# Layer 0's last two FFN output units by thirds, squares added by GpSimd, and layer 1's first norm in single blocks

## What is computed

```python
def _rmsnorm(x, g):
    xf = x.astype(F32)
    y = xf * lax.rsqrt(jnp.mean(xf * xf, axis=-1, keepdims=True) + EPS)
    return (y * g.astype(F32)).astype(x.dtype)
...
        xp = xp + g2p[:, None] * _swiglu(hp, w_ffn_gate[l], w_ffn_up[l], w_ffn_down[l])
        xs = xs + g2s[:, None] * _swiglu(hs, w_ffn_gate[l], w_ffn_up[l], w_ffn_down[l])
...
        hp = _modulate(xp, norm_mix[l], sh1p, sc1p)
        hs = _modulate(xs, norm_mix[l], sh1s, sc1s)
...
            q, k, v = _odd_project(hp, w_in_odd[o])
```

## Time and profile before

| | us |
|---|---|
| median of 3 runs | 3015.53 |
| lowest and highest | 3014.42 and 3015.95 |
| the profiled execution | 3010.81 |
| its span in the trace | 3009.0 |
| PE busy | 2855.7 |
| DVE, POOL, ACT busy | 1745.3, 1539.7, 1007.9 |

### The profile page before, as it was taken

How to read it: one execution, slowest core, us unless ns; L and a number is a source line. 1 busy time by engine, 2 the same in 40 slices (tenths; PEclk the granted TensorE clock), 3 DMA queues, 4 the chain that set the end, 5 groups by cost and what they waited for, 6 DMA issues and landing times. The chain is left out here.

```text
span 3009.0 us, 61068 instructions
## 1 busy us (share of the span) xinstructions
PE 2855.7 (95%) x24985; PEld 2653.3 (88%) x24985; DVE 1745.3 (58%) x3132; ACT 1007.9 (33%) x2102; POOL 1539.7 (51%) x1381
## 2 busy tenths in 40 slices
PE   6999999997789999999999999999999999999998
PEld 4859999765689999999999999956699999999998
DVE  6399999556646644335697400066648543445785
ACT  3351111356434433332232311155525333332222
POOL 2121224464523877776576232144334777775675
PEclk8999999998999999999999999999999999999999
DMA  6716763642241121224222223163221222223321
GB/s 218 253 69 226 249 228 117 183 159 90 94 166 50 64 86 65 86 86 136 87 71 86 81 98 105 53 203 112 69 98 40 82 72 78 86 73 128 122 69 69
DMA packets 192053, 338.85 MB, mean 113 GB/s; under 512 B 27784, under 2 KB 107424, under 8 KB 189920
## 3 DMA queue, kind: packets, MB, share of 16 engines
q1 hardware_dynamic: 138832, 266.50, 26.4%
q10 hardware_dynamic: 52944, 68.45, 6.6%
HBM read 268.30 MB, written 79.49 MB: 116 GB/s over the span
## 5 line engine op out<-in xcount | busy, mean ns | idle before, releaser
L109 PE MATMUL tr_acc<-tr_quad_hi,ah_ring_hi 128*128 128x264 f32 x2432 | 694.7, 286 | 8.3 <-DVE tr_kept L1440 2.2
L733 POOL TENSOR_TENSOR ah_ring_lo<-ah_raw,ah_ring_hi 128x512 fp32r<-128x512 f32 (+2 forms) x426 | 579.7, 1368 | 236.9 <-ACT ah_ring_hi L1140 146.1
L111 PE MATMUL tr_acc<-tr_quad_hi,ah_ring_lo 128*128 128x264 f32 x2432 | 692.9, 285 | 0.0
L110 PE MATMUL tr_acc<-tr_quad_lo,ah_ring_hi 128*128 128x264 f32 x2432 | 690.5, 284 | 0.0
L109 PEld LDWEIGHTS tr_acc<-tr_quad_hi,ah_ring_hi 128*128 128x128 f32 x2432 | 458.6, 189 | 10.5 <-DVE tr_kept L1440 2.6
L110 PEld LDWEIGHTS tr_acc<-tr_quad_lo,ah_ring_hi 128*128 128x128 f32 x2432 | 458.8, 189 | 0.1
L111 PEld LDWEIGHTS tr_acc<-tr_quad_hi,ah_ring_lo 128*128 128x128 f32 x2432 | 458.3, 188 | 0.0
L2898 DVE CUSTOM_DVE_ANT_0 pc_prob<-pc_dots,pc_bias 128x640 f32<-128x640 f32 (+4 forms) x128 | 79.0, 655 | 286.2 <-POOL pc_bias L2701 261.8
L1760 DVE TENSOR_SCALAR_CACHE_REDUCE f_q<-score,choose_trial 128x384 bf16<-128x384 f32 (+6 forms) x224 | 242.2, 1146 | 1.1
L2064 POOL CAST f_w_hi<-f_raw 128x512 fp32r<-128x512 f32 x66 | 46.6, 705 | 375.9 <-DMA f_raw<-in_w_dram 204.7
L731 POOL CAST ah_ring_hi<-ah_raw 128x512 fp32r<-128x512 f32 (+1 forms) x114 | 72.3, 635 | 295.2 <-PE tr_acc L111 281.1
(11 more groups left out here) (409 smaller groups left out, 7447.6 us busy)
## 6 DMA issues: line engine op xcount, KB each, us to landing
f_ada_w<-in_w_ada_dram SPq DMA_DIRECT2D x48, 1024.0 KB, 5.8
scratch_inner<-tr_kept ACTq DMA_DIRECT2D x88, 264.0 KB, 2.2
ah_raw<-in_w_gate_dram SPq DMA_DIRECT2D x44, 512.0 KB, 3.5
ah_raw<-in_w_up_dram SPq DMA_DIRECT2D x44, 512.0 KB, 4.5
ah_raw<-in_w_down_dram SPq DMA_DIRECT2D x64, 256.0 KB, 3.2
f_raw<-in_w_dram SPq DMA_DIRECT2D x24, 512.0 KB, 8.2
out_z_dram<-f_stage ACTq DMA_DIRECT2D x60, 176.0 KB, 1.9
out_z_dram<-tr_value ACTq DMA_DIRECT2D x48, 176.0 KB, 1.9
```

What stands on the lines that cost most here:

```text
L109: pe.matmul(out, w_hi, hi, start=start, stop=False, skip_group_check=onto)
L110: pe.matmul(out, w_hi, lo, start=False, stop=False, skip_group_check=onto)
L111: return pe.matmul(out, w_lo, hi, start=False, stop=stop, skip_group_check=onto)
L733: pool.tensor_tensor(lo[:, 0:width], own, hi[:, 0:width].bitcast(F32), ALU.subtract).then_inc(w_ready, 1)
```

## The change

The last two down units of layer 0, u and v here, run together by thirds: u0 v0 u1 v1 u2 v2. The sum of third 0 stands behind v1 and the sum of third 1 behind v2. The norm's event is split: ("inverse", 0, t) is the reciprocal, and ("norm", k, t) is one block. Third 0's blocks 0 to 2 stand behind v1's residual, 3 and 4 behind u2's, 5 to 7 behind v2's; then third 1's norm. What follows (a, sum 2, norm 2, b and so on) keeps its order. All 21 additions of squares of layer 0 go from DVE to POOL, with four buffers sq; in POOL's list nine of them (the two first units of the part) stand ahead of a's splits and the other twelve ahead of b's. ACT's `upper_halves(t)` becomes `upper_half(k, t)`, and DVE's `norm(t)` becomes `inverse_of(t)` and `norm(k, t)`. The last layer keeps its order.

```diff
--- before.py
+++ after.py
@@ -198,15 +198,21 @@
                 self.events += [("sum", 0, 2)] + [("scale", k, 1) for k in (3, 4)] + [("spread", 0, 2)]
                 self.events += [("scale", k, 1) for k in range(5, KD)] + [("scale", k, 2) for k in range(KD)]
                 u = end
-            elif u == end - 1:
-                for t in range(2):
+            elif not last and u == end - 2:
+                v, a, b = u + 1, u + 2, u + 3
+                for t in range(3):
                     self.events += [("mm", u, t), ("end", u, t)]
-                self.events += [("sum", 0, 0), ("norm", 0, 0), ("mm", u, 2), ("end", u, 2), ("sum", 0, 1), ("norm", 0, 1)]
-                a, b = u + 1, u + 2
-                self.events += [("mm", a, 0), ("sum", 0, 2), ("end", a, 0), ("norm", 0, 2), ("mm", b, 0), ("end", b, 0)]
+                    if t == 2:
+                        self.events += [("norm", k, 0) for k in (3, 4)]
+                    self.events += [("mm", v, t)] + [("sum", 0, t - 1)] * (t > 0) + [("end", v, t)]
+                    if t == 1:
+                        self.events += [("inverse", 0, 0)] + [("norm", k, 0) for k in range(3)]
+                self.events += [("norm", k, 0) for k in range(5, KD)] + [("inverse", 0, 1)] + [("norm", k, 1) for k in range(KD)]
+                self.events += [("mm", a, 0), ("sum", 0, 2), ("end", a, 0), ("inverse", 0, 2)]
+                self.events += [("norm", k, 2) for k in range(KD)] + [("mm", b, 0), ("end", b, 0)]
                 for t in range(1, 3):
                     self.events += [("mm", a, t), ("end", a, t), ("mm", b, t), ("end", b, t)]
-                u += 3
+                u += 4
             else:
                 for t in range(len(TOK_TILES) if self.units[u][0] == "tok" else 3):
                     self.events += [("mm", u, t), ("end", u, t)]
@@ -393,10 +399,10 @@
         sq = [at(f"sq{b}", [P, THIRD], F32, KEPT_AT + 4 * THIRD * b) for b in range(2)]
         total = [at(f"total{t}", [P, THIRD], F32, KEPT_AT + 4 * THIRD * (2 + t)) for t in range(3)]
         rstd = [at(f"rstd{b}", [P, THIRD], F32, KEPT_AT + 4 * THIRD * (5 + b)) for b in range(2)]
+        sq += [at(f"sq{b}", [P, THIRD], F32, KEPT_AT + 4 * THIRD * ((3 if last else 5) + b)) for b in (2, 3)]
         if last:
-            sq += [at(f"sq{b}", [P, THIRD], F32, KEPT_AT + 4 * THIRD * (3 + b)) for b in (2, 3)]
             token_root = at("token_root", [P, 3, 3], F32, KEPT_AT + 4 * THIRD * 7)
-        late_adds = max(plan.add_no.values()) - 1
+        late_adds = max(plan.add_no.values()) + (-1 if last else 1)
         eps = m.sb(f"{name}_eps", [P, 1])
         pair = [m.ps(f"{name}_acc{b}", [P, 2, 512]) for b in range(4)]
         ring_pairs = [pair[1], pair[2], pair[0], pair[3]]
@@ -806,6 +812,18 @@
                 combine(u)
                 for n in range(3, 7):
                     split(u, n, factor_of(u, n))
+            def add_squares(u, t):
+                for a in range(2):
+                    if units[u][1] or a:
+                        i = plan.add_no[u, t, a]
+                        if i >= late_adds:
+                            return
+                        pool.wait_ge(squared, plan.square_no[u, t, a] + 1)
+                        if i:
+                            pool.wait_ge(pool_summed, i)
+                        pool.tensor_tensor(total[t][:], total[t][:], sq[i % 4][:], ALU.add).then_inc(pool_summed, 1)
+
+            ends = [(u, t) for what, u, t in events if what == "end" and u in plan.squared]
             for i in range(plan.slot_no[DOWN_FIRST, 0], len(plan.slots)):
                 u, n = plan.slots[i]
                 kind, j, first, nk = units[u]
@@ -816,6 +834,9 @@
                         mix_seventh({4: 1, 12: 3, 14: 4}[u - DOWN_FIRST])
                     seventh_factors(u)
                     continue
+                if not last and u in (plan.z_first, plan.z_first + 1):
+                    for at in ends[0:6] if u == plan.z_first else ends[6:]:
+                        add_squares(*at)
                 loaded(pool, u)
                 if kind == "down":
                     for a in range(2):
@@ -824,21 +845,9 @@
                     for n in range(4):
                         split(u, n, raw[u % 2][:, KH * P * n:KH * P * n + KH * P])
 
-            def add_squares(u, t):
-                for a in range(2):
...
             if last:
-                for what, u, t in events:
-                    if what == "end" and u in plan.squared:
-                        add_squares(u, t)
+                for at in ends:
+                    add_squares(*at)
 
         @block.tensor
         def _(pe):
@@ -1023,7 +1032,7 @@
                                          start=True, stop=True)
                     done.then_inc(ssq_ready, 1)
                     return
-                pe.wait_ge(summed, plan.sums_done[t])
+                pe.wait_ge(pool_summed, plan.sums_done[t])
                 if t >= 2:
                     pe.wait_ge(root, t - 1)
                 pe.matmul(pair[3][:, t % 2, 0:THIRD], c.ones[:], total[t][:], start=True, stop=True).then_inc(ssq_ready, 1)
@@ -1221,10 +1230,8 @@
                     act.wait_ge(added, plan.read_no[u, t] + a)
                     if j or a:
                         i = plan.add_no[u, t, a]
-                        if last and i >= 4:
+                        if i >= 4:
                             act.wait_ge(pool_summed, i - 3)
-                        elif not last and i >= 2:
-                            act.wait_ge(summed, i - 1)
                         act.activation(sq[i % len(sq)][:], x[:, 2 * j + a, lo:hi], ACT.Square).then_inc(squared, 1)
                     else:
                         act.activation(total[t][:], x[:, 0, lo:hi], ACT.Square).then_inc(squared, 1)
@@ -1268,16 +1275,15 @@
                 act.activation(rstd[t % 2][:], pair[3][:, t % 2, 0:THIRD], ACT.Sqrt, bias=eps[:, 0:1], scale=1.0 / D
                                ).then_inc(root, 1)
 
-            def upper_halves(t):
-                if t == 0:
+            def upper_half(k, t):
+                if k == t == 0:
                     part_over(act, 4)
-                for k in range(KD):
-                    i = KD * t + k
-                    act.wait_ge(scaled, i + 1)
-                    for lo, hi, s in THIRD_SPANS[t]:
-                        done = act.activation(h_hi_t[:, k, lo:hi], tmp[i % 3][:, lo - THIRD * t:hi - THIRD * t],
-                                              ACT.Identity, bias=shift[:, k, s:s + 1])
-                    done.then_inc(h_hi, 1)
+                i = KD * t + k
+                act.wait_ge(scaled, i + 1)
+                for lo, hi, s in THIRD_SPANS[t]:
+                    done = act.activation(h_hi_t[:, k, lo:hi], tmp[i % 3][:, lo - THIRD * t:hi - THIRD * t],
+                                          ACT.Identity, bias=shift[:, k, s:s + 1])
+                done.then_inc(h_hi, 1)
 
             for b in range(4):
                 for k in range(KD):
@@ -1578,14 +1584,6 @@
                             if i > late_adds:
                                 dve.wait_ge(summed, i - late_adds)
                             dve.tensor_tensor(total[t][:], total[t][:], sq[i % 4][:], ALU.add).then_inc(summed, 1)
-                elif u in plan.squared:
-                    for a in range(2):
-                        if j or a:
-                            i = plan.add_no[u, t, a]
-                            dve.wait_ge(squared, plan.square_no[u, t, a] + 1)
-                            if i:
-                                dve.wait_ge(summed, i)
-                            dve.tensor_tensor(total[t][:], total[t][:], sq[i % 2][:], ALU.add).then_inc(summed, 1)
 
             def lower_half(t, k):
                 i = KD * t + k
@@ -1597,24 +1595,26 @@
                         op0=ALU.add, op1=ALU.subtract)
                 done.then_inc(h_ready, 1)
 
-            def norm(t):
+            def inverse_of(t):
                 dve.wait_ge(root, t + 1)
                 dve.reciprocal(rstd[t % 2][:], rstd[t % 2][:]).then_inc(inverse, 1)
                 dve.wait_ge(inverse, t + 1)
                 if t == 0:
                     part_over(dve, 4)
-                for k in range(KD):
-                    if KD * t + k >= 3:
-                        dve.wait_ge(h_ready, KD * t + k - 2)
-                    for lo, hi, s in THIRD_SPANS[t]:
-                        own = slice(lo - THIRD * t, hi - THIRD * t)
-                        done = dve.scalar_tensor_tensor(out=tmp[(KD * t + k) % 3][:, own], in0=x[:, k, lo:hi],
-                                                        scalar=gain[:, k, s:s + 1], in1=rstd[t % 2][:, own],
-                                                        op0=ALU.mult, op1=ALU.mult)
-                    done.then_inc(scaled, 1)
-                    if k:
-                        lower_half(t, k - 1)
-                lower_half(t, KD - 1)
+
+            def norm(k, t):
```

(33 more changed lines are left out.)

## The result

| | before | changed kernel |
|---|---|---|
| median of 20 runs, us | 3013.98 | 3022.2 |
| lowest and highest | 3009.2 and 3022.9 | 3014.77 and 3030.05 |
| ratio | 1 | 1.0027 (95% interval 1.0019 to 1.0034) |
| span of the profiled execution | 3009.0 | 3023.7 |
| from the part's first square to the last z product | 325.5 | 333.6 |

A forecast was written before the change was run, and what follows sets the result against it. PE, busy 95%, was taken to bound the kernel, with DVE's norm chain ending last at the change. Terms -1.25 + 2.6 = +1.35, +1.7 with the lower clock, taken as +1.5: 3015.53 to 3017.0 us, range 3012.5 to 3021.

The forecast's parts named there:

- The standstill before the sum of third 0: PE after v1 waits about 3.7 us for POOL's additions 9 to 12, queued behind a's four splits.
- Covers: Waits said to cost nothing: weights of a and b (b's covered by 4 us), norms of thirds 1 and 2.
- The first tmp: DVE's norm of third 0: first tmp at 1655.37 instead of 1656.62, a gain of 1.25 us.
- Rival B: PE's clock falls and is low when the second half starts, costing 3.1 us: +4.6, 3020.1; chance 0.18.
- a clock of 0.50 beyond 1667: Sign on PE's granted clock, low after 1667, by which the prediction would be wrong.
- part (3): DVE's norm of third 0: -1.25 us at the first tmp, +2.6 for two residuals, taken as +1.5 with the clock.
- The price of the residuals: Residuals of u2 and v2 between DVE's norm blocks of third 0: 2 x 1.3 = 2.6 us lost.
- part (4): Later work: b's late splits, third 1's and third 2's norms and SP's loads are covered; cost nothing.
- Rival A: POOL is in time for third 0's sum: -2.6 us, 3012.9; chance 0.17 with partial cases.
- Rival C: The change does nothing, as old and new gap match and DVE's chain ends at the same time: 3015.5; chance 0.10.

The follow-up runs named there:

- after_again: The changed kernel run once more, unaltered, beside the others on the same chip; 1.0033 of the time of the kernel before.
- e3_hold_b: The changed kernel, but POOL starts b's four splits only when all eight lower halves of third 0 are written; 1.0022 of the kernel before.
- e1_queue: The changed kernel with POOL's additions 9 to 12 put ahead of unit a's splits; 1.0030 of the kernel before.
- e2_dve_adds: The changed kernel with all 21 additions of squares back on DVE, new order and four buffers kept; 1.0004 of the kernel before.
- e4_idle_adds: The kernel before with eight unneeded additions of 352 columns on POOL from third 0's first norm block on; 1.0015 of the kernel before.

## Why the prediction was wrong

**Right: what PE and POOL do.** The standstill before the sum of third 0 is there, 3.72 us where the sum gave 3.69 (1651.45 - 1647.76), with the four splits between additions 8 and 9, and square 13 waiting for addition 9. Covers held: no wait for weights of a or b, none for third 1's or third 2's norm, and PE is busy without a break for 150 us behind, so the loss is carried on one to one.

**Right in kind, small misses.** The first tmp came 33.70 us behind the first square, where the sum gave 33.0 (1655.37 - 1622.35). The 0.7 is the sum itself: its two matmuls took 1.51 at the lower clock instead of 0.83. I had put that at 0.3. The low clock cost another 0.46 in the last products of the first half (1.11 us from the last lo's end to the second half, 0.65 before) and 0.6 in the first matmuls of the second: this is Rival B's mechanism, at a third of its price of 3.1. The clock was low from 1674.5 to 1681.3, about as long as the 6.3 us that Rival B laid over PE's work, but only the last 1.2 us of it lay there, the rest under DVE's chain. In after_again 3.9 us lay there and cost 1.7. It is one of the signs by which the prediction called itself wrong, a clock of 0.50 beyond 1667: 1674.5 here is 1667.9 in the time of the trace before.

**Wrong: part (3), the step "from the first tmp to the last lo the old chain takes 8.58", with 2.6 for two residuals.** This took its durations from rows in which POOL stood: before the change POOL is idle for 38 us from 1656.8 on, and these were the only rows of L1611 and L1594. Measured: from 1662.69 to 1678.96, 16.27 us instead of 11.2, so 5.1 more. Of the 6.2 by which the second half missed the forecast, this is 5.1, the sum 0.7 and the low clock 0.46. The step failed because it gave DVE's norm steps the length that they have beside an idle POOL. The eight slow steps account for it: 2.7 beside additions 17 to 20 and 2.75 beside b's first two splits, less 0.3 for a wait for ACT and for residuals that were a little shorter than priced. e3_hold_b takes the splits away, and the chain goes from 16.3 to 13.8 us. The price of the residuals was right: they hold DVE for 1.23 each.

The trace before the change did show the mechanism. The same kind of step stands in layer 0's own norm, where a lower half of 528 columns takes 0.76 with POOL idle (three in a row take 2.12 from 950.50 on) and 1.79 here (POOL, then DVE):

```profile
937.38 1.63 POOL L733 TENSOR_TENSOR ah_ring_lo<-ah_raw,ah_ring_hi 128x512 fp32r<-128x512 f32 x1
```

```profile
937.78 1.79 DVE L1416 SCALAR_TENSOR_TENSOR tr_quad_lo<-tr_full,mod,tr_quad_hi 128x528 fp32r<-128x528 f32 x1
```

And on the tile total L1588 took 0.526 or up to 1.430. I wrote that down as "up to 1.430 beside POOL", and used it to shorten POOL's splits once DVE's additions were gone. I did not turn it round and ask what POOL's additions and the splits that they delay would do to DVE's steps, on the one engine that I had just named as the one that ends last. And part (4) called b's late splits free because their readers were covered. Their readers were. Their neighbour on DVE was not: additions 17 to 20, which DVE had made itself, and the first two of b's splits now lie under its norm steps. The third lies under the reciprocal of third 1, which is not slowed, and the fourth under the first tmps behind it.

The Trainium skill has this in the GPSIMD Engine Reference, section 8 (Key points): GpSimd shares its SBUF interfaces with VectorE, with contention against VectorE instructions that have two SBUF inputs. The trace agrees: the two-input steps on SBUF went from 0.57 to 1.25, the residuals with one input in PSUM (1.08) and the reciprocal with one input (2.35) did not change.

**The rivals.** Rival A (POOL in time) did not happen; e1_queue made it happen for that sum and showed that of the gain of 4.65 us at the first tmp 2.7 is eaten by contention. Rival C fell. Rival B's side was right, but its cause, the low clock, has only about 1 us of the loss, 1.7 with the two matmuls of the sum. The chances gave 0.10 to slower by over 0.2%, and no rival had a price for what became slower.

**What stays open.** POOL's additions in the old order, without the order by thirds, were not run, so the share of each part of the change is told only by way of e2_dve_adds. What lies behind the second half (e1_queue's stretch is 332.5 with a second half at 49.2) is the low clock in its first matmuls, 1.35 us there; why the clock stays low for four matmuls in one profile and for ten to thirteen in others is open. The spread of several us ahead of the changed place is seen and not explained.

## What to carry to other kernels

Before work goes from DVE to POOL, or slides along POOL's queue, list which DVE instructions with two SBUF inputs will then run beside it and price both sides at the slower figure, here 1.25 instead of 0.57 for 352 columns beside an addition. Count POOL's instructions there: each of them held up one DVE step, and the longer it was, the longer the step. A wait in a queue is priced by its reader; a busy engine must also be priced by its neighbours. And an earlier start of a chain is worth only what the next sums and banks let through: six orders had their first tmp 3.3 to 5.2 us sooner than before and kept 0.8 us at most.

## What the runs showed of the hardware

DVE's two-input step on SBUF of 352 columns takes 0.57 alone, 0.92 beside a stream of POOL casts or copies of 512 columns, 1.25 beside a stream of POOL additions of 352 and 1.60 beside a POOL lower half of 512. It goes one step to one POOL instruction: the starts are 0.85 us apart beside casts and 1.17 to 1.18 beside additions, on both engines. POOL's additions go from 1.09 to about 1.18 from start to start (9.41 for eight). In e4_idle_adds eight additions, 9.4 us of POOL that nobody waits for, made DVE's chain 5.3 us longer and PE's second half 5.7 later.

The residuals, with one input in PSUM, and the reciprocal, with one input, were not slowed. One input alone is no safe sign: this small step of the kernel before takes 0.171 in the median and 0.917 at 279.59, where a POOL instruction of 1.29 us runs (times in ns, minimum, median and maximum):

```profile
L1781 DVE TENSOR_SCALAR choose_keep<-choose_count x31: 171/171/917, 228.0 to 489.4; 128x7 int32<-128x7 f32 x31
```
